# Three reorderings in a two-block transformer kernel: copies of tile 18 ahead of the heads' root, the last rotary join behind a head's low half, and the sums of x4 one tile further ahead

## The chip, the cores and the metric

The kernel runs on one core of one Trainium2 chip. The metric is the device time of one execution in microseconds (us). Five engines work side by side, each in its own program order, and meet through semaphores: PE (TensorE; its weight loads are shown apart as PEld), DVE (VectorE), ACT (ScalarE), POOL (GpSimd) and SP (SyncE, which issues most DMAs).

## The reference, cut to what matters

Two blocks follow each other on an input of 512 tokens by 1024 columns, all in float32: a gated block with a convolution and a feed-forward layer, and a block with two kinds of attention. The change lies in the second block.

```python
h = rmsnorm(x, g_pre_mix)
q_a, k_a, v_a, q_i, k_i, w_i, q_d, k_d, v_d = split(h @ w_in)
q_a, k_a = apply_rope(q_a), apply_rope(k_a)          # 8 heads of 64
o_a = dsa_attention(q_a, k_a, v_a, q_i, k_i, w_i)     # softmax over the 128 best keys
o_d = diff_attention(q1, q2, k1, k2, v_d, lam)        # 4 heads of 128
o_d = rmsnorm(o_d, g_diff_sub) * (1 - lam_init)       # per head: a root, a factor
x = x + rmsnorm(concat(o_a, o_d) @ w_out, g_post_mix) # this sum is x4
h = rmsnorm(x, g_pre_mlp)
u = relu(h @ w_up)
x = x + rmsnorm((u * u) @ w_down, g_post_mlp)
```

## The kernel before, in words

**Layout and precision.** Activations lie transposed: eight tiles k = 0..7 of 128 partitions by 512 tokens. Each operand of a large product is split into a high part (`xh`, `wh`) and a low part (`xl`, `wl`), so that one product becomes three matmuls (lines L728 to L730, helper `three`). ACT makes the high halves of activations, DVE the low halves, POOL most halves of the weights. Each engine's program is written out by hand; no scheduler moves anything.

**The attention steps.** Attention runs over 32 tiles, 16 of the differential heads (4 heads by 4 token blocks) and 16 of the sparse heads (4 pairs of heads by 4 token blocks). All engines walk through steps n = -2..32. In step n PE issues the scores of tile n+2 (L1179), a piece of some projection (L728 to L730), the transposes of tile n's probabilities (L1193, "turn"), and the product with the values of tile n-1 (L1221 or L1217). The turned tile lies in two PSUM banks, which ACT copies out in `keep_turned(n)` (L1703); PE may turn tile n+1 only into banks that are copied out. DVE does `normalise(n)` (L2533, L2534) and `shift(n+2)` (L2505), ACT the exponentials of tile n+2 (L1688).

**The heads' root.** A finished differential head needs its root of the mean square: PE sums (L826, L828), ACT takes the root in `head_roots` (L1720), which needs another activation table than the exponential and so a table load before and one behind it, DVE inverts in `head_factors` (L2540), PE spreads the factor over the partitions in `norm_spread` (L849), DVE multiplies (L2573), ACT makes the high half (L1730), DVE the low half (L2551). Heads 2 and 3 share one root; head 3's spread waits for head 2's low half, since both use one PSUM bank.

**The rotary moves.** The q and k of the sparse heads are rotated on DVE in groups g. The last one, g = 9, holds half of k (`ka`, head pairs 2 and 3). `rope_even(9)` (L2402) and `rope_odd(9)` (L2408) write the two halves of `ropey`; when the second is there, SP moves the result to its place by eight DMAs, since it must change partitions:

```python
            def move_rope(g, dst, m):

                sp.wait_ge(rope_ready, g + 1)
...
                        sp.dma_start(dst[p0:p0 + 32, 2 * m + hh // 2], ropey[32 * hh:32 * hh + 32, g % 2, part]
                                     ).then_inc(rope_moved[g % 2], 16)
```

PE asks for these moves in `scores`, ahead of the scores of tile 24 (`DIFF_TILES + 2 * TB`), which it issues in step 22 (L1179), for all eight DMAs of every group:

```python
                if n in (DIFF_TILES, DIFF_TILES + 2 * TB):
                    for half_moved in rope_moved:
                        pe.wait_ge(half_moved, 16 * 8 * (4 if n == DIFF_TILES else 5))
```

**The output projection's pieces.** `out2_piece` puts parts of `out2` between the tiles from step 19 on. Piece 3, the second one of step 21, multiplies head 3 and waits for its low half.

**x4.** Behind the attention, DVE builds x4 tile by tile in three rotating PSUM banks: `x4_scale(k)` (an L1843 multiply), `x4_sum(k)` (L2639), `x4_low(k)` (L1862). ACT makes the high half (L1774), a copy (L1770) and a square (L1410). PE's `several` takes tile k in nine matmuls, six with the high half (L786, L787) and then three with the low half (L794).

Of the kernel before, what the change touches and what calls it, by code (L numbers as in the profile page):

```python
# [35 lines left out]
KT = D // P  # L36
# [50 lines left out]
E_QK = E_VA + 4  # L87
# [40 lines left out]
def tile_of(n):  # L128

    if n < DIFF_TILES:  # L130
        return True, n // TB, n % TB
    return False, (n - DIFF_TILES) // TB, n % TB
# [16 lines left out]
def turns_to(n):  # L149

    return n + 1 if n < DIFF_TILES else DIFF_TILES + 2 * (n - DIFF_TILES + 1)


def turns_of(n):

    return range(1 if n < DIFF_TILES else 2)
# [61 lines left out]
def build(nc, a):  # L218
    ctx = ExitStack()
    with ctx:  # L220
# [1154 lines left out]
        def _(act):  # L1375
# [304 lines left out]
            def exp(n):  # L1680

                diff, h, tb = tile_of(n)
                N = (tb + 1) * P
                for e in range(2):
                    slot = 2 * (n % 3) + e
                    act.wait_ge(shifted, 2 * n + e + 1)
                    total = sums0[:, n:n + 1] if diff and e == 0 else soft[:, 8 + slot:9 + slot]
                    A(probs[slot][:, 0:N], probs[slot][:, 0:N], ACT.Exp, scale=-1.0, bias=soft[:, slot:slot + 1],  # L1688
                      accum_out=total).then_inc(exp_done, 1)

            def keep_turned(n):

                diff, h, tb = tile_of(n)
                N = (tb + 1) * P
                if n >= 2:
                    act.wait_ge(pv_done, n - 1)
                else:
                    act.wait_ge(score_step, 24)
                if n == DIFF_TILES:
                    act.wait_ge(pv_done, DIFF_TILES)  # L1700
                for e in turns_of(n):
                    act.wait_ge(turned, turns_to(n - 1) + e + 1)
                    A(pT[n % 2][e][:, 0:N], bank[turn_bank[e]][:, 0:N], ACT.Copy).then_inc(pT_ready, 1)  # L1703

            def keep_output(h):

                act.wait_ge(pv_done, 4 * (h + 1))
                if h == 0:
                    act.wait_ge(ki_moved, 64)
                    act.wait_ge(rope_ready, 6)  # L1710
                if h >= 2:
                    act.wait_ge(sums_done, 6 + h)
                A(kept[h][:], bank[1 if h == 3 else 6][:], ACT.Copy).then_inc(o_kept, 1)
                act.wait_ge(o_kept, h + 1)
                A(sq[h % 2][:], kept[h][:], ACT.Square).then_inc(head_sq, 1)

            def head_roots(n):

                act.wait_ge(sums_done, n // 8 * 2 + 7)
                A(sd[:, 0:8], NB[:, 0:8], ACT.Sqrt).then_inc(sd_ready, 1)  # L1720

            def step(n):
                if 0 <= n < TILES:
                    keep_turned(n)
                if n in HIGH_AT:

                    h = HIGH_AT[n]
                    act.wait_ge(chunk_done, C_OUT2)
                    act.wait_ge(bc_used, 9 + h)
                    A(xh[:, 4 + h], kept[h][:] if h < 2 else NB[:], ACT.Copy).then_inc(xh_ready, 1)  # L1730
                ends_head = n % 4 == 0 and 1 <= n // 4 <= DIFF_HEADS
                if n == DIFF_TILES:
                    keep_output(DIFF_HEADS - 1)
                if n + 2 < TILES:
                    exp(n + 2)
                for piece in pieces_at(n):
                    o, k = divmod(piece, 4)
                    if k == 3:
                        if o % 2:
                            act.wait_ge(chunk_done, C_OUT2 + o // 2 + 1)  # L1740
                        else:
                            act.wait_ge(even_out_done, o // 2 + 1)
                        A(ym[:, o], bank[(2, 7)[o % 2]][:], ACT.Copy).then_inc(evacuated, 1)
                if ends_head and n < DIFF_TILES:
                    keep_output(n // 4 - 1)
                if n in (9, 17):
                    head_roots(n)
                if n > DIFF_TILES + TB and n % TB == 1 or n == TILES:

                    pair = (n - DIFF_TILES - 1) // TB - (n != TILES)  # L1750
                    act.wait_ge(pv_done, DIFF_TILES + TB * (pair + 1))
                    A(xh[:, pair], bank[(6, 1)[pair % 2]][:], ACT.Copy).then_inc(xh_ready, 1)
# [79 lines left out]
        def _(dve):  # L1832
# [571 lines left out]
            def rope_odd(g, out0):  # L2404
                cs = rope_tokens(g)
                dve.wait_ge(evacuated, out0 + 2)
                dve.wait_ge(rope_step, 3 * g + 3)
                V.tensor_tensor(ropey[:, g % 2, 1, cs], tmp[2][:, cs], tmb[3][:, cs], ALU.add).then_inc(rope_ready, 1)  # L2408
# [127 lines left out]
            def head_factors(b):  # L2536

                dve.wait_ge(sd_ready, 9 + b)
                dve.wait_ge(bc_done, 8 + 2 * b)
                V.reciprocal(rn[:, 0:8], sd[:, 0:8]).then_inc(rn_ready, 2)  # L2540

            def step(n):
                if 0 <= n < TILES:
                    normalise(n)
                if n in LOW_AT:
                    h = LOW_AT[n]
                    if h == 2:
                        dve.wait_ge(xl_ready, 3 * KT + 2)
                        lows[0] += 2
                    dve.wait_ge(xh_ready, lows[0] + 1)  # L2550
                    V.tensor_tensor(xl[:, 4 + h], NB[:], xh[:, 4 + h].bitcast(F32), ALU.subtract).then_inc(xl_ready, 1)  # L2551
                    lows[0] += 1
                if n in (4, 8):
                    top_max()
                if n in (-1, 5, 9):
                    top_replace()
                if n == 12:
                    top_mask()
                if n == 17:
                    qk_second(9)  # L2560
                if n == 18:
                    rope_even(9)
                if n == 19:
                    head_factors(1)
                if n + 2 < TILES:
                    shift(n + 2)
                if n == 12:
                    head_factors(0)
                if n in SPREAD_AT:

                    h = SPREAD_AT[n]
                    dve.wait_ge(bc_done, 9 + h)
                    V.scalar_tensor_tensor(out=kept[h][:] if h < 2 else NB[:], in0=kept[h][:], scalar=diff_gain[:],  # L2573
                                           in1=NB[:], op0=ALU.mult, op1=ALU.mult).then_inc(bc_used, 1)
                if n > DIFF_TILES + TB and n % TB == 2:
                    pair = (n - DIFF_TILES) // TB - 1
                    low_of(pair, bank[(6, 1)[pair % 2]][:])
# [10 lines left out]
            for n in range(-2, TILES + 1):  # L2588
                step(n)
                if n == -2:  # L2590
                    top_max()
                if n in (0, 4, 8, 13):
                    qk_first({0: 6, 4: 7, 8: 8, 13: 9}[n])
                if n in (2, 6, 10):
                    qk_second({2: 6, 6: 7, 10: 8}[n])
                if n in (3, 7, 11):
                    qk_join({3: 6, 7: 7, 11: 8}[n])
                if n == 19:
                    rope_odd(9, E_QK + 6)
            for k in range(KT // 2):  # L2600
                x3_scale(k)
            low_of(3, bank[1][:])
# [19 lines left out]
            def x4_scale(k):  # L2622

                if k == 0:
                    dve.wait_ge(bc_done, 13)
                if k >= 3:
                    dve.wait_ge(x4_kept, k - 2)
                dve.wait_ge(ym_gained, k + 1)
                mul(x4_bank[k % 3][:], ym[:, k], NB[:]).then_inc(y_scaled if k < KT - 1 else bc_used, 1)

            def x4_sum(k):

                dve.wait_ge(x3_ready, k + 1)
                out = x4_bank[k % 3][:]
                if k < KT - 1:
                    dve.wait_ge(y_scaled, k + 1)
                else:
                    dve.wait_ge(bc_used, 13)
                V.tensor_tensor(out, out, x[:, k], ALU.add).then_inc(x4_ready, 1)  # L2639
# [5 lines left out]
            x4_scale(0)  # L2645
            x4_sum(0)
            x4_scale(1)
            for k in range(KT):
                x4_low(k)
                if k < KT - 1:  # L2650
                    x4_sum(k + 1)
                if k < KT - 2:
                    x4_scale(k + 2)
            squares[0] += KT
            plain_run(C_FF2, 13, 4, pairs_of(2)[0], "pre_mlp")
            dve.wait_ge(rn_ready, 14)
# [142 lines left out]
```

## Time and profile before

| | |
|---|---|
| median of 3 runs | 1131.68 us (1131.12 to 1131.96) |
| the profiled execution's own time | 1131.43 us |
| its span in the trace | 1129.5 us |
| PE busy | 1113.7 us (99%) |
| DVE, POOL, ACT busy | 708.6, 685.0, 391.4 us |
| granted TensorE clock | 0.999 of full speed |

The span is what the trace covers; the execution's own time has 1.9 us around it. In the rows, "busy" of PE counts matmuls whose ends are modelled and which overlap; PEld, the weight loads, shows better when PE is held. Behind an instruction stands in brackets how long its engine sat idle before it and what ended that.

### The profile page before, as it was taken

How to read it: one execution, taken by the hardware profiler on the slowest of the kernel's cores; microseconds unless marked ns; L12 is line 12 of the kernel's file. 1: busy time of each engine (PE TensorE's matmuls, PEld its weight loads, DVE VectorE, ACT ScalarE, POOL GpSimd, SP SyncE). 2: the span in 40 equal slices, each digit the busy share in tenths (PEclk: the TensorE clock that was granted, in tenths of full speed). 3: DMA queues.
4: the chain of work that ended last, by engine and by line, in shares of the span. 5: the costliest groups of instructions: out<-in, count | busy, mean ns of one | idle time of the engine just before them, and what ended most of it. 6: DMA issues, size and time to landing. Idle time of an engine off the chain costs nothing.

```text
span 1129.5 us, 17246 instructions
## 1 busy us (share of the span) xinstructions
PE 1113.7 (99%) x6167; PEld 941.9 (83%) x6167; DVE 708.6 (63%) x1386; ACT 391.4 (35%) x799; POOL 685.0 (61%) x459
## 2 busy tenths in 40 slices
PE   7999999999999999999999999999999999999997
PEld 5888788998889998888778777677899888999885
DVE  4999868851148854447789777666888113885023
ACT  5134355540015531111201346655665000554012
POOL 7869947486645586666556433135857763568662
PEclk9999999999999999999999999999999999999999
DMA  7322223243313243334333232112124822235411
GB/s 251 130 76 65 85 75 94 75 142 103 100 66 111 96 152 110 93 93 149 112 112 101 83 87 68 38 57 75 58 92 134 184 94 65 93 106 181 159 52 74
DMA packets 52251, 115.54 MB, mean 102 GB/s; under 512 B 21840, under 2 KB 22480, under 8 KB 52176
## 3 DMA queue, kind: packets, MB, share of 16 engines
q1 hardware_dynamic: 31200, 105.40, 29.1%
q10 hardware_dynamic: 20976, 9.15, 3.4%
q8 instruction: 46, 0.75, 0.3%
q14 instruction: 29, 0.24, 0.1%
HBM read 105.09 MB, written 4.19 MB: 97 GB/s over the span
## 4 chain that ended last, share of the span: by engine, by line
PE 92%; DVE 5%; ACT 2%; issue 1%; DMA 0%; DVEq 0%; SPq 0%; ACTq 0%
PE bank L728 21%; PE bank L730 20%; PE bank L729 20%; PE bank L1345 5%; PE bank L1346 5%; PE bank L1344 5%; DVE bank L1952 3%; PE bank L1179 2%; PE bank L761 1%; PE bank L762 1%; PE bank L760 1%; PE bank L794 1%; PE bank L786 1%; PE bank L787 1%; PE bank L1193 1%
## 5 line engine op out<-in xcount | busy, mean ns | idle before, releaser
L543 POOL TENSOR_TENSOR wl<-raw,wh 128x1024 fp32r<-128x1024 f32 x140 | 337.5, 2411 | 11.7
L540 POOL TENSOR_SCALAR wh<-raw 128x1024 fp32r<-128x1024 f32 x140 | 150.3, 1074 | 264.8 <-PE bank L730 148.2
L728 PE MATMUL bank<-xh,wh 128*128 128x512 f32 (+2 forms) x680 | 237.7, 350 | 0.0
L730 PE MATMUL bank<-xh,wl 128*128 128x512 f32 (+2 forms) x680 | 232.5, 342 | 0.0
L729 PE MATMUL bank<-xl,wh 128*128 128x512 f32 (+2 forms) x680 | 232.2, 341 | 0.0
L728 PEld LDWEIGHTS bank<-xh,wh 128*128 128x128 f32 x680 | 128.3, 189 | 29.3 <-issue 16.4
L730 PEld LDWEIGHTS bank<-xh,wl 128*128 128x128 f32 x680 | 128.3, 189 | 14.5
L1538 ACT ACTIVATE wh<-bank 128x512 fp32r<-128x512 f32 x96 | 52.2, 596 | 252.5 <-DVE bank L2197 109.0
L729 PEld LDWEIGHTS bank<-xl,wh 128*128 128x128 f32 x680 | 128.4, 189 | 13.0 <-issue 0.2
L728 PE MATMUL bank<-uh,wh 128*128 128x512 f32 x288 | 112.8, 392 | 0.0
L730 PE MATMUL bank<-uh,wl 128*128 128x512 f32 x288 | 112.1, 389 | 0.0
L729 PE MATMUL bank<-ul,wh 128*128 128x512 f32 x288 | 112.1, 389 | 0.0
L729 PE MATMUL bank<-t_low,wh 128*128 128x256 f32 x384 | 107.6, 280 | 0.0
L730 PE MATMUL bank<-t_high,wl 128*128 128x256 f32 x384 | 107.3, 280 | 0.0
L728 PE MATMUL bank<-t_high,wh 128*128 128x256 f32 x384 | 107.2, 279 | 0.0
L1345 PE MATMUL bank<-wl,uh 128*128 128x512 f32 x240 | 93.4, 389 | 0.0
L1346 PE MATMUL bank<-wh,ul 128*128 128x512 f32 x240 | 93.4, 389 | 0.0
L1344 PE MATMUL bank<-wh,uh 128*128 128x512 f32 x240 | 93.4, 389 | 0.0
L1843 DVE TENSOR_TENSOR bank<-bank,rb 128x512 f32<-128x512 f32 x16 | 11.2, 700 | 110.9 <-PE bank L730 110.9
L2212 DVE TENSOR_TENSOR wl<-bank,wh 128x512 fp32r<-128x512 f32 x96 | 63.4, 684 | 25.3 <-ACT wh L1538 24.7
L664 POOL TENSOR_SCALAR wh<-raw 128x512 fp32r<-128x512 f32 x24 | 14.9, 622 | 102.0 <-PE bank L730 89.0
L728 PEld LDWEIGHTS bank<-t_high,wh 128*128 128x128 f32 x384 | 72.8, 189 | 0.0
(343 smaller groups left out, 2271.8 us busy)
## 6 DMA issues: line engine op xcount, KB each, us to landing
raw<-wstream SPq DMA_DIRECT2D x188, 512.0 KB, 3.5
x<-xT SPq DMA_DIRECT2D x8, 256.0 KB, 4.8
x4rows<-x_rows ACTq DMA_DIRECT2D x4, 512.0 KB, 9.6
out<-x4rows SPq DMA_DIRECT2D x8, 256.0 KB, 2.0
qd<-ropey ACTq DMA_DIRECT2D x16, 64.0 KB, 2.1
kd<-ropey ACTq DMA_DIRECT2D x16, 64.0 KB, 2.1
qa<-ropey SPq DMA_DIRECT2D x16, 64.0 KB, 2.0
ka<-ropey SPq DMA_DIRECT2D x16, 64.0 KB, 2.0
```

The source lines that it names most:

```text
L540: nc.gpsimd.tensor_scalar(wh[c][:], raw[c][:], 1.0, 1.0, ALU.mult, ALU.mult).then_inc(high_ready, 1)
L543: nc.gpsimd.tensor_tensor(wl[c][:], raw[c][:], wh[c][:].bitcast(F32), ALU.subtract).then_inc(split_ready, 1)
L728: mm(out, wh_, mh, start=start, stop=False)
L729: mm(out, wh_, ml, start=False, stop=False)
L730: return mm(out, wl_, mh, start=False, stop=stop)
L1179: mm(bank[4 + e][:, score_columns(m)], q[r, h, tb * P:tb * P + P], k[r, h, 0:(tb + 1) * P], start=True, stop=True).then_inc(scores_done, 1)
L1344: mm(out, uh[:, f, ts], wh[s][:, ws], start=f == 0, stop=False)
L1345: mm(out, uh[:, f, ts], wl[s][:, ws], start=False, stop=False)
L1346: last = mm(out, ul[:, f, ts], wh[s][:, ws], start=False, stop=f == 15)
L1538: A(wh[slot_of(p, role)][:, 512 * part:512 * part + 512], bank[7 - made % 2][:], ACT.Copy).then_inc(sum_rounded, 1)
L1952: ins = V.scalar_tensor_tensor(out=out, in0=src, scalar=w, in1=acc, op0=ALU.mult, op1=ALU.add)
L2212: V.tensor_tensor(wl[slot][:, at], bank[7 - made % 2][:], wh[slot][:, at].bitcast(F32), ALU.subtract).then_inc(sum_ready, 1)
```

## The change: what it does

It moves four things. On ACT, the root of heads 2 and 3 stood at the end of step 17 and stands in step 18 behind the copies of turned tile 18. On DVE, the inversion of that root stood ahead of `shift(21)` and stands behind it; and `rope_odd(9)` stood behind step 19 and stands in step 20, behind the low half of head 2 and ahead of `shift(22)`. In the x4 stage, `x4_sum(k)` stood behind `x4_low(k - 1)` and stands two tiles ahead, right behind `x4_scale(k)`. No instruction is added or taken away.

```diff
@@ ACT: step(n)
                 if 0 <= n < TILES:
                     keep_turned(n)
+                if n == 18:
+                    head_roots(17)
...
-                if n in (9, 17):
+                if n == 9:
                     head_roots(n)
@@ DVE: step(n)
-                if n == 19:
-                    head_factors(1)
+                if n == 20:
+                    rope_odd(9, E_QK + 6)
                 if n + 2 < TILES:
                     shift(n + 2)
-                if n == 12:
-                    head_factors(0)
+                if n in (12, 19):
+                    head_factors(n // 19)
...
-                if n == 19:
-                    rope_odd(9, E_QK + 6)
@@ DVE: x4
             x4_scale(0)
             x4_sum(0)
             x4_scale(1)
+            x4_sum(1)
             for k in range(KT):
                 x4_low(k)
-                if k < KT - 1:
-                    x4_sum(k + 1)
                 if k < KT - 2:
                     x4_scale(k + 2)
+                    x4_sum(k + 2)
```

On ACT, around the root (L1703 copies a turned tile, L1720 is the root, L1688 the exponentials):

```order
 L1688 ACTIVATE probs_123,soft<-probs_123,soft 128x512 x2
+L1703 ACTIVATE tmp_91<-bank 128x384
+L1703 ACTIVATE vd<-bank 128x384
 L1720 ACT_TABLE_LOAD
 L1720 ACTIVATE sd<-bank 128x8
-L1703 ACTIVATE tmp_91<-bank 128x384
-L1703 ACTIVATE vd<-bank 128x384
 L1688 ACT_TABLE_LOAD
```

The two copies of tile 18 went ahead of the table load and the root; both table loads are still there.

On DVE, steps 19 and 20 before the change (L2540 the inversion, L2505 shifts, L2573 head 2 times its factor, L2408 the second rotary join, L2533 and L2534 `normalise(20)`, L2551 head 2's low half):

```order
L2540 RECIPROCAL rn<-sd 128x8
L2505 ISA probs_123,soft<-bank,work 128x256
L2505 ISA soft 128x1
L2505 ISA probs_123,soft<-bank,work 128x256
L2505 ISA soft 128x1
L2573 SCALAR_TENSOR_TENSOR bank<-rb,diff_gain,bank 128x512
L2408 TENSOR_TENSOR ropey<-tmp_90,tmb_95 128x512
L2533 RECIPROCAL soft<-soft 128x1
L2534 TENSOR_SCALAR probs_151<-probs_151,soft 128x128
L2533 RECIPROCAL soft<-soft 128x1
L2534 TENSOR_SCALAR probs_152<-probs_152,soft 128x128
L2551 TENSOR_TENSOR xl<-bank,xh 128x512
```

The same place of the changed kernel, from the inversion on, where every line number is two higher:

```order
L2542 RECIPROCAL rn<-sd 128x8
L2575 SCALAR_TENSOR_TENSOR bank<-rb,diff_gain,bank 128x512
L2535 RECIPROCAL soft<-soft 128x1
L2536 TENSOR_SCALAR probs_151<-probs_151,soft 128x128
L2535 RECIPROCAL soft<-soft 128x1
L2536 TENSOR_SCALAR probs_152<-probs_152,soft 128x128
L2553 TENSOR_TENSOR xl<-bank,xh 128x512
L2410 TENSOR_TENSOR ropey<-tmp_90,tmb_95 128x512
L2507 ISA probs_123,soft<-bank,work 128x384
```

The four shift instructions went ahead of the inversion, and the join moved past five instructions, among them the low half that waits for ACT.

On DVE, the start of the x4 stage before (L1843 scales, L2639 sums, L1862 makes the low half):

```order
L1843 TENSOR_TENSOR bank<-ym,bank 128x512
L2639 TENSOR_TENSOR bank<-bank,x 128x512
L1843 TENSOR_TENSOR bank<-ym,bank 128x512
L1862 SCALAR_TENSOR_TENSOR xl<-bank,cols,xh 128x512
L2639 TENSOR_TENSOR bank<-bank,x 128x512
L1843 TENSOR_TENSOR bank<-ym,bank 128x512
L1862 SCALAR_TENSOR_TENSOR xl<-bank,cols,xh 128x512
```

and in the changed kernel:

```order
L1845 TENSOR_TENSOR bank<-ym,bank 128x512
L2639 TENSOR_TENSOR bank<-bank,x 128x512
L1845 TENSOR_TENSOR bank<-ym,bank 128x512
L2639 TENSOR_TENSOR bank<-bank,x 128x512
L1864 SCALAR_TENSOR_TENSOR xl<-bank,cols,xh 128x512
L1845 TENSOR_TENSOR bank<-ym,bank 128x512
L2639 TENSOR_TENSOR bank<-bank,x 128x512
L1864 SCALAR_TENSOR_TENSOR xl<-bank,cols,xh 128x512
```

Each sum now stands directly behind the scaling whose result it reads, and the first low half has one more sum ahead of it.

## Rows read from the trace of the kernel before

**Rows 1.** The page: busy time of each engine, share of the span, instructions.

```profile
PE 1113.7 (99%) x6167; PEld 941.9 (83%) x6167; DVE 708.6 (63%) x1386; ACT 391.4 (35%) x799; POOL 685.0 (61%) x459
```

**Rows 2.** PE's waits, whole span: total us, times, longest us.

```profile
PE bank L786 <- ACT xh L1418: 5.6, 1, 5.6
PE bank L1193 <- ACT tmp L1703: 0.5, 1, 0.5
```

**Rows 3.** Timeline, ACT: start us, us, instruction, [idle before <-releaser].

```profile
702.80 1.28 ACT L1720 ACT_TABLE_LOAD   x1
704.10 0.18 ACT L1720 ACTIVATE sd<-bank 128x8 f32<-128x8 f32 x1
704.17 0.48 ACT L1703 ACTIVATE tmp<-bank 128x384 f32<-128x384 f32 x1
704.54 0.50 ACT L1703 ACTIVATE vd<-bank 128x384 f32<-128x384 f32 x1
705.06 1.28 ACT L1688 ACT_TABLE_LOAD   x1
...
708.09 0.59 ACT L1730 ACTIVATE xh<-bank 128x512 fp32r<-128x512 f32 x1
```

**Rows 4.** Timeline, DVE, steps 19 to 21.

```profile
703.62 0.49 DVE L2534 TENSOR_SCALAR probs<-probs,soft 128x512 f32<-128x512 f32 x1
704.36 0.20 DVE L2540 RECIPROCAL rn<-sd 128x8 f32<-128x8 f32 x1 [0.25 <-ACT sd L1720]
...
707.00 0.69 DVE L2408 TENSOR_TENSOR ropey<-tmp,tmb 128x512 f32<-128x512 f32 x1
...
708.79 0.69 DVE L2551 TENSOR_TENSOR xl<-bank,xh 128x512 fp32r<-128x512 f32 x1 [0.31 <-ACT xh L1730]
709.40 0.55 DVE L2505 CUSTOM_DVE_ANT_0 probs<-bank,work 128x384 f32<-128x384 f32 x1
...
711.92 0.69 DVE L2551 TENSOR_TENSOR xl<-bank,xh 128x512 fp32r<-128x512 f32 x1
```

**Rows 5.** Timeline, PE's weight loads, steps 19 to 22.

```profile
704.77 0.85 PEld L1193 LDWEIGHTS bank<-ident,probs 128*128 128x128 f32 x8 [0.91 <-DVE probs L2534]
705.59 0.47 PEld L849 LDWEIGHTS bank<-ident,rn 128*128 128x128 f32 x4
...
709.53 0.41 PEld L849 LDWEIGHTS bank<-ident,rn 128*128 128x128 f32 x4 [0.71 <-DVE xl L2551]
...
712.77 0.19 PEld L728 LDWEIGHTS bank<-xh,wh 128*128 128x128 f32 x1
...
714.59 0.52 PEld L1179 LDWEIGHTS bank<-ka,qa 64*128 64x128 f32 x8 [0.17 <-issue]
```

**Rows 6.** Timeline, SP's queue: the move of group 9.

```profile
707.72 4.95 SPq L469 DMA_DIRECT2D ka<-ropey  x8
```

**Rows 7.** The same move by line: duration ns, first and last start; landing.

```profile
L469 SPq DMA_DIRECT2D ka<-ropey x8: 512/591/592, 707.7 to 712.1; - x8
...
DMA to landing us min/median/max: 1.9/2.0/2.0
```

**Rows 8.** SP's queue by line, 679 to 685 us: landing of group 8's moves.

```profile
DMA to landing us min/median/max: 1.9/2.0/3.0
```

**Rows 9.** Timeline of the x4 stage.

```profile
781.57 0.69 DVE L1843 TENSOR_TENSOR bank<-ym,bank 128x512 f32<-128x512 f32 x1 [0.74 <-PE bank L849]
...
782.37 0.70 DVE L2639 TENSOR_TENSOR bank<-bank,x 128x512 f32<-128x512 f32 x1
...
784.87 0.19 PEld L787 LDWEIGHTS bank<-xh,wl 128*128 128x128 f32 x1
...
785.10 0.65 PEld L794 LDWEIGHTS bank<-xl,wh 128*128 128x128 f32 x3
...
785.94 0.75 DVE L1862 SCALAR_TENSOR_TENSOR xl<-bank,cols,xh 128x512 fp32r<-128x512 f32 x1 [0.16 <-ACT xh L1774]
...
786.61 0.69 DVE L2639 TENSOR_TENSOR bank<-bank,x 128x512 f32<-128x512 f32 x1
...
787.20 0.68 DVE L1843 TENSOR_TENSOR bank<-ym,bank 128x512 f32<-128x512 f32 x1
...
798.62 0.75 DVE L1862 SCALAR_TENSOR_TENSOR xl<-bank,cols,xh 128x512 fp32r<-128x512 f32 x1 [0.76 <-ACT xh L1774]
```

## The prediction, made before the changed kernel ran

> **What bounds the kernel now.** The page comes first: PE is busy 1113.7 us, 99% of the span [rows 1]. A microsecond taken from another engine is therefore worth nothing unless PE stands waiting for it, and a microsecond by which PE is held comes out at the end almost whole. The view of waits shows how few holds are left: one of 5.6 us at the start, where the first input is fetched, and otherwise half a microsecond here and there [rows 2]. So I read the timelines around the places of the change and asked for each instruction of PE what releases it and how long before PE got there that was ready. Since matmuls overlap in the rows, I use the weight loads (PEld), whose idle time shows a hold plainly.
>
> In steps 18 to 20 a chain through ACT holds PE twice. ACT works without a break: table load, root, two copies of tile 18, table load, exponentials, two copies of tile 19, head 2's high half [rows 3]. PE's loads first sit idle 0.91 us before tile 19 is turned [rows 5]. That row names DVE, but DVE was done at 703.62 + 0.49 = 704.11 us [rows 4]; last came the bank that ACT's first copy of tile 18 frees at 704.17 + 0.48 = 704.65, and the view of waits says so too [rows 2, 3]. It waits again, 0.71 us, for head 2's low half at 709.53, and that low half started when ACT's high half was done [rows 3 to 5].
>
> **The root behind the copies.** ACT's own sum over the moved piece: before, from 702.80 to the end of the second table load at 705.06 + 1.28 = 706.34, 3.54 us. After: copies 0.37 (the distance of the two starts) + 0.50, table load 1.28, root 0.18, table load 1.28, with gaps of 0.02 as between these rows, together 3.67 us [rows 3]. The difference of 0.13 us is that a copy could start 0.07 us behind the root, while a table load starts only when the instruction before it has ended. So the exponentials, the copies of tile 19 and head 2's high half come 0.13 us later: the high half at 708.22, the low half at 708.92, PE's second spread at 709.66.
>
> What does PE win? It can turn tile 19 when DVE's second half is there, about 704.2 instead of 704.77. But next in its order is the spread of head 2's factor. The root now starts at 702.80 + 0.87 + 0.02 + 1.28 + 0.02 = 704.99, the inversion 0.26 us behind its start as before (704.36 - 704.10), so at 705.25, and it lasts 0.20: the spread can start near 705.49, where it started at 705.59 [rows 3 to 5]. The shift that now stands ahead of the inversion is done by then: DVE is free from 704.11 on, and even two shifts of 384 columns would take 1.1 us at 0.55 each, these have 256 [rows 4]. The hold of 0.91 us is thus not removed, it moves 0.6 us down PE's program; and the 0.1 us won is lost again at the second spread, which ACT's chain decides. Worth of this part: 0.13 us lost.
>
> **The join behind the low half.** This decides the forecast. `rope_odd(9)` started at 707.00 [rows 4]. It will start one instruction behind the low half: 708.92 + 0.61 (the distance 708.79 to 709.40 in the same rows) = 709.53, so 2.53 us later. Three things follow.
>
> First, everything DVE has behind it moves by 0.61 + 0.13 = 0.74 us: `shift(22)`, head 3's product, and head 3's low half, which ended at 711.92 + 0.69 = 712.61. PE asks for it at 712.77 [rows 4, 5], a margin of 0.16 us. It will end at 713.35 while PE gets there at 712.90, so PE is held about 0.5 us more.
>
> Second, SP's eight DMAs hang on the join. Before, the first was issued at 707.72, 0.72 us behind the join's start, the last at 707.72 + 4.95 - 0.59 = 712.08, 4.36 us behind the first, and each lands 2.0 us behind its issue: the last at 714.1 [rows 6, 7]. PE needs all of them for the scores of tile 24 and issues these at 714.59 after no more than 0.17 us of idle time that the view calls issue, as at many such places [rows 5]. The margin was therefore about 0.5 us, and it was never seen as a wait. After: 709.53 + 0.72 + 4.36 + 2.0 = 716.61 for the last landing, and some 0.06 us for PE to go on: 716.67. Against 714.59 that is **2.08 us later**. The 0.13 and 0.5 us from above do not add up with it: they let PE arrive at about 715.0 and wait 1.6 us there instead of 2.2. SP issues the eight in one piece, with nothing of its weight loads between them [rows 6].
>
> Third, could it be caught up? Behind the wait, DVE and ACT will stand ready, but PE is not waiting for them in the steps after; only such a wait could give time back. POOL and the weight DMAs run ahead of PE and do not set it. So 2.08 us stay.
>
> **The sums of x4.** Before, DVE's low half of tile k is followed by the sum of k+1 (0.67 us behind its start), the sum releases ACT's high half, and this the next low half: a loop of (798.62 - 785.94) / 6 = 2.113 us [rows 9]. Each low half waits 0.16 us for it, so this loop, and not DVE's own work, sets the pace. PE's nine matmuls go at 0.23 us each in this stage (784.87 to 785.10), 2.08 us. So PE is held about 0.03 us per tile. After, high halves come early, and DVE's own pace counts: low to scale 0.67, scale to sum 0.80, sum to next low 0.61. The 0.80 is read from 781.57 to 782.37, where the sum reads what the scaling just wrote; a pair without that stands 0.59 to 0.61 apart (786.61 to 787.20, and 708.79 to 709.40) [rows 4, 9]. That makes 2.08 us, no slower than PE. The first low half comes later, with one dependent sum in front: 781.57 + 0.80 + 0.61 + 0.80 + 0.61 = 784.39, done at 785.14 against PE's load at 785.10: a hold of 0.1 us. The seven following tiles give back 0.03 each, 0.2 us; together with the first tile's change-over 0.1 to 0.2 us are won. I take 0.15. The bounds: 0.3 us lost, if the dependent pairs cost 0.05 us more in each of seven tiles, and 0.3 us won, if PE is never held.
>
> The Trainium skill, "VectorE: DVE Perf Modes", section "The DRAIN you can't avoid", states that between chained vector instructions "the semaphore costs nothing extra here". By that, the dependent pair would take 0.61 us like any other, DVE's pace would be 1.89 us, and this term 0.3 us instead of 0.15. The row of 0.80 speaks against it for this pair, and I go by the row.
>
> **Sum.** 1131.43 us is the profiled execution's own time, 1129.5 of span and 1.9 around it. Plus 2.08, minus 0.15: 1133.36. The median of the runs stands 0.25 us above that execution, so I forecast 1131.68 + 1.93 = **1133.6 us**. What a measurement of this kernel can tell from no change is about 0.2%, 2.26 us: slower means above 1133.94. The forecast is a real loss that just stays within that bound.
>
> **The rivals.**
> - *The moves are hidden* (1 in 10). PE would have to get to tile 24 later than I reckon, or DMAs land faster. For it: no wait on a DMA shows anywhere near before. Against: the margin is two subtractions from rows, and the shift is five times as large. Then the 0.13 and 0.5 us remain: 1131.68 + 0.63 - 0.15 = 1132.2 us.
> - *Slower by more than the bound* (about 1 in 4 in all). The move of group 8 had one DMA that took 3.0 us instead of 2.0 [rows 8]. If the last DMA of group 9 is such a one, its later landing goes straight to PE: 1133.6 + 1.0 = 1134.6 us. It decides from 0.35 us of lateness on. Against: group 9's eight DMAs all took 1.9 to 2.0 us, [rows 7]. That gives 1 in 10; the rest is my own error of some 0.4 us on the main case.
> - *Faster* (1 in 20). The turn of tile 19, up to 0.6 us earlier, holds if the factor's spread comes as early too, which needs a root on ACT ahead of 704.5; and the moves are hidden. With x4's 0.3 that is 0.9 us: 1130.8 us. It decides where the inversion starts before 704.4, and ACT's order all but excludes that. Only with further gains that I see no row for would it pass 0.2%.
>
> **How the numbers follow.** Main case 0.75, with a range of its own of 1133.1 to 1134.2; hidden 0.10; a late landing 0.10; faster 0.05. The range goes from 1132.0, which takes in the hidden case, to 1134.7, which takes in the late landing; outside are the faster case and the tails. Of the main case, 0.15 lies above 1133.94, and of the late landing nearly all: slower 0.25. Faster by over 0.2% gets 0.03, and the rest, 0.72, lies within.
>
> **What the changed kernel's profile would show.** The join (now L2410) starts near 709.5 us and SP's eight moves near 710.25. PEld's L1179 of tile 24 starts near 716.7 with an idle time of about 1.8 us before it, and the view of waits has a line of PE or PEld on a DMA of `ka` that was not there. The turn of tile 19 starts near 704.2, and the first L849 behind it at 705.5 with an idle time of 0.6 us. The piece of `out2` at 712.77 starts near 713.4. In the x4 stage the loads of L794 stand 2.08 to 2.10 us apart. The forecast is wrong if L1179 of tile 24 shows no wait, if the join starts earlier than 709, or if the last landing lies more than 0.4 us from 716.6.

## The result, and the profile after

The changed kernel takes 1133.13 us (median of 22 runs, 1132.77 to 1134.47), before 1131.36 us (22 runs, 1131.08 to 1131.96): 1.77 us more, a ratio of 1.0016 with a 95% interval of 1.0010 to 1.0022. The forecast was 1133.6 us, 1.93 us more. Nineteen of the 22 runs lie between 1132.77 and 1133.47 us; three stand apart at 1134.28 to 1134.47; the paragraph on the rivals, near the end, comes back to them.

The page of the changed kernel: span, and busy time by engine, which answer to [rows 1]:

```profile
span 1131.5 us, 17246 instructions
PE 1114.3 (98%) x6167; PEld 942.7 (83%) x6167; DVE 709.2 (63%) x1386; ACT 391.8 (35%) x799; POOL 684.2 (60%) x459
```

The engines do the same work as before in a span 2.0 us longer. Not all of the 2.0 is the change's. A weight load ahead of every edit tells how the two traces stand to each other; before, then after:

```profile
699.87 0.30 PEld L826 LDWEIGHTS bank<-scaled_eps,ident 128*128 128x128 f32 x2 [0.17 <-issue]
```

```profile
700.22 0.30 PEld L826 LDWEIGHTS bank<-scaled_eps,ident 128*128 128x128 f32 x2 [0.17 <-issue]
```

This execution was 0.35 us late already, so 0.35 us comes off every time of it that is set against the rows of before. By the two profiled executions the change costs 1133.44 - 1131.43 - 0.35 = 1.66 us.

PE's weight loads in the changed kernel, timeline, answering to [rows 5]:

```profile
704.25 1.02 PEld L1193 LDWEIGHTS bank<-ident,probs 128*128 128x128 f32 x8
705.77 0.41 PEld L849 LDWEIGHTS bank<-ident,rn 128*128 128x128 f32 x4 [0.50 <-issue]
...
709.86 0.41 PEld L849 LDWEIGHTS bank<-ident,rn 128*128 128x128 f32 x4 [0.90 <-DVE xl L2553]
...
713.59 0.19 PEld L728 LDWEIGHTS bank<-xh,wh 128*128 128x128 f32 x1 [0.54 <-DVE xl L2553]
...
716.87 0.55 PEld L1179 LDWEIGHTS bank<-ka,qa 64*128 64x128 f32 x8 [1.76 <-issue]
```

There are four things to see. The 0.91 us idle before the turn of tile 19 is gone. But 0.50 us of idle time stands now before the first spread, where there was none, and 0.90 us before the second, where 0.71 stood. A hold of 0.54 us for head 3's low half is new. And the scores of tile 24 start at 716.87 - 0.35 = 716.52 instead of 714.59, 1.93 us later, behind 1.76 us of idle time. The view calls this idle time "issue": it names no DMA as what ended it. The rows of the move itself show what did, SP's queue as a timeline and then by line:

```profile
710.43 4.95 SPq L469 DMA_DIRECT2D ka<-ropey  x8
```

```profile
L469 SPq DMA_DIRECT2D ka<-ropey x8: 513/591/592, 710.4 to 714.8; - x8
...
DMA to landing us min/median/max: 1.9/2.0/2.0
```

The last of the eight is issued at 710.43 + 4.95 - 0.59 = 714.79 and lands 2.0 us later, at 716.79; PE goes on at 716.87. DVE and ACT around it, from the timelines:

```profile
709.11 0.69 DVE L2553 TENSOR_TENSOR xl<-bank,xh 128x512 fp32r<-128x512 f32 x1 [0.96 <-ACT xh L1732]
709.72 0.68 DVE L2410 TENSOR_TENSOR ropey<-tmp,tmb 128x512 f32<-128x512 f32 x1
```

```profile
702.94 0.19 ACT L1688 ACTIVATION_READ_ACCUMULATOR probs<-probs,soft 128x1 f32 x1
703.03 0.47 ACT L1703 ACTIVATE tmp<-bank 128x384 f32<-128x384 f32 x1
703.40 0.48 ACT L1703 ACTIVATE vd<-bank 128x384 f32<-128x384 f32 x1
703.89 1.28 ACT L1720 ACT_TABLE_LOAD   x1
705.19 0.18 ACT L1720 ACTIVATE sd<-bank 128x8 f32<-128x8 f32 x1
705.38 1.28 ACT L1688 ACT_TABLE_LOAD   x1
```

The join starts 0.61 us behind the low half. It stands behind 0.96 us in which DVE does nothing but wait for ACT.

### The profile page after: what moved, and what is told of

Same layout as the page of the kernel before. It is cut to its first block, busy times and chain, and to the rows that moved or that the text cites. A ratio compares the mean times of both kernels' runs of the same rounds, so it can differ in the third digit from the quotient of the medians.

```text
span 1131.5 us, 17246 instructions
## 1 busy us (share of the span) xinstructions
PE 1114.3 (98%) x6167; PEld 942.7 (83%) x6167; DVE 709.2 (63%) x1386; ACT 391.8 (35%) x799; POOL 684.2 (60%) x459
## 4 chain that ended last, share of the span: by engine, by line
PE 91%; DVE 5%; issue 1%; ACT 1%; DMA 0%; DVEq 0%; SPq 0%; ACTq 0%
PE bank L728 20%; PE bank L730 20%; PE bank L729 20%; PE bank L1346 5%; PE bank L1344 5%; PE bank L1345 5%; DVE bank L1954 3%; PE bank L1179 2%; PE bank L794 1%; PE bank L786 1%; PE bank L787 1%; PE bank L760 1%; PE bank L762 1%; PE bank L761 1%; PE bank L1193 1%
```

## The experiments

Each experiment was timed side by side with the kernel before, which had a median of 1131.68 us in the first set (33 runs, experiments 1 to 4), 1131.61 in the second (30, experiments 5 to 8), 1131.54 in the third (21, experiments 9 and 10). The interval of each ratio reaches about 0.09%, 1.0 us, to either side. What is smaller than that is read from the traces; the medians can only support it.

**1. The join alone.** Only these lines on the kernel before:

```diff
+                if n == 20:
+                    rope_odd(9, E_QK + 6)
                 if n + 2 < TILES:
                     shift(n + 2)
...
-                if n == 19:
-                    rope_odd(9, E_QK + 6)
```

> Only the second rotary join moves behind head 2's low half; root and x4 stay as before. If the moves of group 9 are what PE waits for, the join starts at 708.79 + 0.61 = 709.4 us, the last of the eight DMAs lands near 716.5, and the scores of tile 24 start near 716.5 instead of 714.6: about 1.9 us more than before, 1133.3 us. The rival, that only DVE's later shift and head 3's later low half hold PE, gives 0.5 us, 1131.9 us, and no idle time ahead of the scores of tile 24.

Measured: 1133.96 us (11 runs, 1133.16 to 1135.14), ratio 1.0023 (1.0014 to 1.0032). PE's weight load of tile 24's scores:

```profile
716.65 0.55 PEld L1179 LDWEIGHTS bank<-ka,qa 64*128 64x128 f32 x8 [1.75 <-issue]
```

The join alone brings the whole loss, with the idle time at the forecast place. The rival of the low half alone would have ended at 1131.9 us. Six runs stand at 1133.16 to 1133.96, around 1133.56 us, which is 1.9 us more than before as expected; five stand at 1134.76 to 1135.14, and they lift the median.

**2. The root alone.** The two edits of `head_roots` and the two of `head_factors`, nothing else.

> Only the root of heads 2 and 3 moves behind the copies of tile 18, with the inversion behind the shift; join and x4 stay as before. By the sum of ACT's own work PE's second spread starts 0.13 us later and nothing else changes: 1131.5 us. The rival, that the earlier turn of tile 19 gives PE time that stays, gives up to 0.6 us less: 1130.8 us.

Measured: 1131.63 us (11 runs), ratio 1.0 (0.9991 to 1.0009). Nothing measurable, either way. The 0.6 us rival falls; whether 0.1 us is won or lost can't be told from runs, but the trace tells it:

```profile
703.82 1.02 PEld L1193 LDWEIGHTS bank<-ident,probs 128*128 128x128 f32 x8
705.36 0.41 PEld L849 LDWEIGHTS bank<-ident,rn 128*128 128x128 f32 x4 [0.51 <-issue]
...
709.45 0.41 PEld L849 LDWEIGHTS bank<-ident,rn 128*128 128x128 f32 x4 [0.91 <-DVE xl L2553]
...
714.51 0.52 PEld L1179 LDWEIGHTS bank<-ka,qa 64*128 64x128 f32 x8 [0.17 <-issue]
```

The turn of tile 19 starts 0.95 us earlier than in [rows 5] (of which this execution is 0.07 early as a whole), and at tile 24 nothing is left of it: 714.51 + 0.07 = 714.58 against 714.59. The hold moved past the turn, as forecast.

**3. The sums of x4 alone.** Only the four lines of the x4 stage.

> Only the sums of x4 move. The changed kernel's trace has PE's low-half loads 2.054 us apart where they stood 2.117 apart: if that is the sums' doing alone, this kernel is 0.4 us faster than before, 1130.95 us. The forecast's term was 0.15 us, 1131.2 us. If the gain in the changed kernel's trace was given back later, no change: 1131.36 us.

Measured: 1131.14 us (11 runs, 1130.82 to 1131.89), 0.54 us under before, ratio 0.9995 (0.9986 to 1.0004). The interval takes in no change, so the gain is read from the trace. PE's loads of the low halves, first and last tile:

```profile
785.65 0.58 PEld L794 LDWEIGHTS bank<-xl,wh 128*128 128x128 f32 x3
...
800.00 0.64 PEld L794 LDWEIGHTS bank<-xl,wh 128*128 128x128 f32 x3
```

That is (800.00 - 785.65) / 7 = 2.05 us a tile, as in the changed kernel. Before, the same loads stand (799.92 - 785.10) / 7 = 2.117 us apart, and DVE's loop in [rows 9] takes 2.113. From the first load of the stage to the first behind it, it is 800.68 - 784.32 = 16.36 us against 16.77 before: 0.41 won.

**4. The changed kernel without the join's move.**

> The changed kernel with the join alone put back behind step 19. If the join carries the whole loss, what is left is root and x4: 0.13 lost and 0.4 won, 1131.1 us, and no idle time ahead of the scores of tile 24. If the root's part carries some of the loss, as the rival has it, it stays above 1131.5 us.

Measured: 1131.12 us (11 runs, 1130.73 to 1131.44), ratio 0.9996 (0.9987 to 1.0005), with 0.17 us of idle time before the scores of tile 24, as before the change. Its median is 2.0 us under the changed kernel's. By the medians the parts add up: 2.28 - 0.05 - 0.54 = 1.69 us from experiments 1 to 3, against 1.77 for all together. That it is so close is partly luck, since five of 11 runs stand in the upper group in experiment 1 and three of 22 in the changed kernel; with the lower groups alone it is 1.88 - 0.59 = 1.29 against 1.71, which the intervals of 1.0 us allow too.

**5. The join later still.** The changed kernel with

```diff
-                if n == 20:
-                    rope_odd(9, E_QK + 6)
                 if n + 2 < TILES:
                     shift(n + 2)
+                if n == 20:
+                    rope_odd(9, E_QK + 6)
```

> The changed kernel with the join one step further back, behind shift(22), which takes DVE 0.95 us. If the time follows the join through the eight DMAs, one for one, the last landing and the scores of tile 24 come 0.95 us later than in the changed kernel: 0.95 us more than its 1133.1 us, 1134.1 us, while head 3's low half stays where it is. If the loss comes from head 3's low half, no change from 1133.1 us.

Measured: 1135.57 us (8 runs), ratio 1.0031 (1.0020 to 1.0042). The median is 2.4 us above the changed kernel where 0.95 was expected. But the runs fall in two groups: two at 1133.97 and 1133.98, 0.9 us above the 1133.07 of the changed kernel's lower nineteen and so as expected, and six at 1135.32 to 1135.63. The profiled execution took 1135.62 us. The new idle time is there:

```profile
717.50 0.55 PEld L1179 LDWEIGHTS bank<-ka,qa 64*128 64x128 f32 x8 [2.70 <-issue]
```

2.70 - 1.76 = 0.94 us more: PE's wait follows the join one for one. The rest of the loss lies behind it. The view of stretches, first two long ones and then three short ones (us; busy time and count of PE, PEld, DVE, ACT, POOL; granted clock; DMA share; GB/s):

```profile
716.00:720.00 4.00, 2.47 (x12) 1.84 (x13) 1.40 (x7) 1.58 (x4) 0.00 (x0) 0.83 0.13 33
720.00:724.00 4.00, 4.00 (x22) 3.02 (x21) 1.61 (x7) 1.28 (x5) 0.00 (x0) 0.74 0.00 0
```

```profile
718.00:719.00 1.00, 1.00 (x7) 0.60 (x5) 0.43 (x5) 0.00 (x0) 0.00 (x0) 0.84 0.00 0
719.00:720.00 1.00, 1.00 (x3) 0.74 (x3) 0.96 (x5) 0.00 (x0) 0.00 (x0) 0.50 0.00 0
722.00:723.00 1.00, 1.00 (x9) 0.69 (x9) 0.01 (x1) 0.28 (x1) 0.00 (x0) 0.95 0.00 0
```

The granted clock is 0.83 and then 0.74 of full speed, where it is 1.00 in the same stretches of the kernels before and changed. By the microsecond it is still 1.00 while PE is idle and until 718, then 0.84, 0.50 in each of 719 to 722, 0.95 behind that, and 1.00 again. What is missing from full speed there adds up to 0.16 + 3 x 0.50 + 0.05 = 1.71 us, and the upper group stands 1.6 us above the lower. The matmuls there, from PE's timeline, the first being the scores of tile 24:

```profile
717.53 0.93 PE L1179 MATMUL bank<-ka,qa 64*128 64x128 f32 x8 [2.49 <-issue]
...
719.18 0.63 PE L730 MATMUL bank<-xh,wl 128*128 128x512 f32 x1
719.60 0.63 PE L728 MATMUL bank<-xh,wh 128*128 128x512 f32 x1
720.03 0.63 PE L729 MATMUL bank<-xl,wh 128*128 128x512 f32 x1
```

The last three start 0.43 us apart instead of 0.23: the lower of the two levels, 1.2 GHz. The matmuls themselves had been idle for 2.49 us; the 2.70 is the idle time of the loads. So there is an expensive kind of run which the DMAs' landing does not explain; all eight landed after 2.0 us here too.

**6. The join ahead of head 2's low half.** The changed kernel with `rope_odd(9, E_QK + 6)` in step 20 in front of the low half, where DVE waits.

> The changed kernel with the join one step forward, ahead of head 2's low half, where DVE stands idle 0.96 us for ACT. Nothing behind it gets later, and the join starts some 0.9 us later than before the change instead of 2.5. The margin of the moves was about 0.45 us, so PE should wait 0.5 us for them; with 0.4 us won in the x4 stage: 1131.7 us where before is 1131.6. The rival, a delay by DVE's order alone, gives the full gain of x4: 1131.2 us.

Measured: 1131.40 us (11 runs, 1131.06 to 1132.17), ratio 0.9998 (0.9989 to 1.0007). PE is idle 0.47 us before the scores of tile 24, of which 0.17 is usual:

```profile
715.77 0.55 PEld L1179 LDWEIGHTS bank<-ka,qa 64*128 64x128 f32 x8 [0.47 <-issue]
```

A hold of 0.3 us, where 0.5 was expected: against the weight load ahead of the edits the join starts 0.73 us later than before the change and not 0.9, which overdraws a margin of 0.43. Head 3's low half holds nobody. The median lies between the two readings of the expectation, 0.2 to 0.3 us from either; the trace decides for the wait.

**7. The even half's moves early.** The changed kernel, and in `move_rope` for g = 9 only, the four DMAs of the even half are issued first, behind a wait for `rope_even`, and the four of the odd half behind the join:

```diff
-                sp.wait_ge(rope_ready, g + 1)
+                if g < 9:
+                    sp.wait_ge(rope_ready, g + 1)
...
-                for hh in range(4):
-                    for part in range(2):
+                for part, hh in [(p, q) for q in range(4) for p in range(2)] if g < 9 else \
+                        [(p, q) for p in range(2) for q in range(4)]:
+                        if g == 9 and hh == 0:
+                            sp.wait_ge((rope_step, rope_ready)[part], (3 * g + 3, g + 1)[part])
```

> The changed kernel, with group 9's four moves of the even half issued as soon as that half is there, some 8 us earlier, and only four behind the join. The join stays late. The last landing comes four issues of 0.63 us earlier, 2.5 us, and so ahead of PE: no idle time at the scores of tile 24. Left are the hold of about 0.5 us for head 3's low half and x4's 0.4: 1131.6 us where before is 1131.6. Whatever the DMAs do to the spread of single runs should be gone as well: no runs 1.3 us above the others. If the late join costs by another way, 1133.1 us remain.

Measured: 1131.50 us (11 runs, 1131.19 to 1131.78), ratio 0.9999 (0.9990 to 1.0008): 1.6 us under the changed kernel with the join as late as there, and no run stands apart. The hold for head 3's low half is still there, the idle time before the scores is back at 0.17 us (all lines stand three lower in this kernel):

```profile
713.05 0.19 PEld L731 LDWEIGHTS bank<-xh,wh 128*128 128x128 f32 x1 [0.54 <-DVE xl L2556]
...
714.74 0.52 PEld L1182 LDWEIGHTS bank<-ka,qa 64*128 64x128 f32 x8 [0.17 <-issue]
```

This is the sharpest test: the programs of PE, DVE and ACT are untouched, and only the times at which SP issues the moves differ.

**8. Both.** Experiments 6 and 7 together.

> Both: the join ahead of head 2's low half, and the even half's moves early. Neither head 3's low half nor the moves are late, so what is left is the gain of x4 and of the root's order: 0.5 us under before, 1131.1 us where before is 1131.6, like the changed kernel with the join put back.

Measured: 1130.97 us (11 runs, 1130.62 to 1131.33), ratio 0.9995 (0.9986 to 1.0004) to before. By its median it is the best of all, 0.64 us under before, and 2.2 under the changed kernel; its interval to before takes in no change.

**9. PE kept busy ahead of the wait, join behind shift(22).** Experiment 5's kernel with two products of constants, added work that no result uses, ahead of PE's wait:

```diff
             def step(n):

+                if n == 22:
+                    for _ in range(2):
+                        mm(NB[:], ones[:], mask[:], start=True, stop=True)
                 if n + 2 < TILES:
                     scores(n + 2)
```

> The kernel with the join behind shift(22), and two products of constants (ones times mask, 128x512, nobody reads them) on PE ahead of the scores of tile 24, where PE stood idle 2.7 us. In the x4 stage three such products kept PE busy 2.7 us, so two fill some 1.8 us of the idle time. If the runs at 1135.6 us come from TensorE's clock going down to the 1.2 GHz level behind the idle time (granted clock 0.83 and 0.74 in the eight microseconds behind it, in the profile of one such run), they are gone and all runs stand near 1134.0 us. If they come from late DMA landings, they stay: PE waits for the same moves.

Measured: 1134.01 us, all eleven runs between 1133.81 and 1134.57; not one at 1135.3 or above, where there had been six of eight. PE waits for the same moves and resumes at the same time, 717.51 against 717.50. By the weight loads it is idle for 1.37 us before that instead of 2.70; by the matmuls, which show what the two products fill, for 0.57 us instead of 2.49:

```profile
714.99 1.98 PE L1264 MATMUL bank<-mask,ones 128*128 128x512 f32 x4
717.55 0.93 PE L1179 MATMUL bank<-ka,qa 64*128 64x128 f32 x8 [0.57 <-issue]
```

```profile
717.51 0.55 PEld L1179 LDWEIGHTS bank<-ka,qa 64*128 64x128 f32 x8 [1.37 <-issue]
```

The granted clock of 720 to 724 us is 1.00. So the 1.6 us of the upper group are the clock's, and without PE's idle time they do not come. That idle time alone does not decide it: two of the eight runs of experiment 5 had no such loss. What decides between runs of one kernel is not shown.

**10. The same with the join alone.** Experiment 1's kernel with one such product.

> The join alone moved (root and x4 as before), with one such product ahead of the scores of tile 24, where PE stood idle 1.75 us; it fills about 0.9 us. Five of eleven runs of that kernel stood 1.3 us above the others. If the clock is the cause, those are fewer or gone and the median comes down to about 1133.6 us; if it is not, about half of the runs stay near 1135 us.

Measured: 1133.72 us (11 runs, 1133.11 to 1134.66). Nine runs lie at 1133.11 to 1133.81, two at 1134.33 and 1134.66; without the product five of eleven stood at 1134.76 or above. The matmuls are idle for 0.48 us before the scores instead of 1.54. The result goes the expected way, but eleven runs are few, and two runs remain above the others whose cause is not shown: their mean granted clock, 0.999, is no lower than the others'. In experiment 1 the clock does not settle it either: 0.996 to 0.998 in the five upper runs, 0.997 to 0.999 in the six lower ones.

## Why the prediction was right

**The number.** Forecast were 1133.6 us, measured 1133.13, 0.5 us less. 0.32 us of that is the starting point: the kernel before takes 1131.36 us by its 22 runs and not the 1131.68 of three. The rest is the change itself, 1.77 us by the medians and 1.66 by the traces where 1.93 was forecast. By the traces the terms are 1.93 us lost at the moves (forecast 2.08) and 0.37 won in the x4 stage (forecast 0.15), and some 0.1 us more lost, which no term names.

**The bound and the place.** That a hold of PE comes out at the end whole is confirmed by experiments 4 and 7, which take the hold away and with it 2.0 and 1.6 us of the median. One sign did not come: the view of waits has no line of PE on a DMA of `ka`. It lists the hold under "issue".

**The root behind the copies.** The mechanism held: the turn of tile 19 earlier, the hold moved down to the spreads, nothing won at the end. The turn came at 704.25 - 0.35 = 703.90 and not at 704.2: its first loads did not wait for DVE's second half, which ended at 703.98 + 0.49 - 0.35 = 704.12. The term was mis-sized. I took 0.13 us lost; in experiment 2 the second spread starts at 709.45 + 0.07 = 709.52 against 709.53, so nothing. I had started the copies at 702.80, the table load's start. Before the change the instruction ahead of the table load was this:

```profile
702.59 0.19 ACT L1688 ACTIVATION_READ_ACCUMULATOR probs<-probs,soft 128x1 f32 x1
```

The table load started 0.21 us behind the start of that reading of the accumulator, at its end. In the changed kernel the copy starts 0.09 us behind it (702.94 to 703.03), while it still runs. The 0.12 us that the copy gains ahead of the root make up for the 0.13 lost behind it.

**The join.** Forecast: join at 709.53, last landing 716.61, scores of tile 24 at 716.67, some 1.8 us of idle time, 2.08 us lost. Measured, with the 0.35 taken off: 709.37, 716.44, 716.52, 1.76 us, 1.93 lost. The difference of 0.15 is nearly all the root's term again, which stood in this chain. Experiment 5 moved the join by 0.95 and PE's start by 0.94; experiment 6 moved it forward and the hold shrank to 0.3; experiment 7 left the join and removed the hold. The hold for head 3's low half was forecast at 0.5 us and is 0.54, and as forecast it does not add up with the wait for the moves: in experiment 7, where no such wait follows, the trace has the hold of 0.54 us and the median is 0.4 to 0.5 us above experiments 4 and 8.

**The sums of x4.** This term was the furthest off in proportion: 0.15 us won by forecast, and by the traces more than my upper bound of 0.3. PE's loads of the stage, the first of it and the first behind it, before:

```profile
783.84 0.19 PEld L786 LDWEIGHTS bank<-xh,wh 128*128 128x128 f32 x1 [0.56 <-ACT xh L1774]
...
800.61 0.19 PEld L728 LDWEIGHTS bank<-xh,wh 128*128 128x128 f32 x1
```

and in the changed kernel, with the last tile:

```profile
786.19 0.19 PEld L786 LDWEIGHTS bank<-xh,wh 128*128 128x128 f32 x1 [0.56 <-ACT xh L1776]
...
787.52 0.59 PEld L794 LDWEIGHTS bank<-xl,wh 128*128 128x128 f32 x3
...
799.85 0.65 PEld L794 LDWEIGHTS bank<-xl,wh 128*128 128x128 f32 x3
800.53 0.19 PEld L786 LDWEIGHTS bank<-xh,wh 128*128 128x128 f32 x1
...
801.90 0.64 PEld L794 LDWEIGHTS bank<-xl,wh 128*128 128x128 f32 x3
802.59 0.19 PEld L728 LDWEIGHTS bank<-xh,wh 128*128 128x128 f32 x1
```

16.77 us before, 16.40 after: 0.37 won. The first low half holds PE for 0.07 us more (787.52 - 786.19 against 785.10 - 783.84), as forecast; the seven tiles behind it give back 0.063 each and not 0.03. The step that failed is "PE's nine matmuls go at 0.23 us each in this stage (784.87 to 785.10), 2.08 us", with that pace taken as the same before and after. In tiles 2 to 8 the last five high-half loads stand on average 0.234 us apart before and 0.228 after; nine of these are 2.10 and 2.05 us. So only some 0.02 us a tile is the hold that went away, and the rest is PE's pace itself. Why that changed is open.

What sets the pace now is DVE, as its timeline in the changed kernel shows:

```profile
787.38 0.68 DVE L1845 TENSOR_TENSOR bank<-ym,bank 128x512 f32<-128x512 f32 x1
788.17 0.70 DVE L2639 TENSOR_TENSOR bank<-bank,x 128x512 f32<-128x512 f32 x1
788.78 0.74 DVE L1864 SCALAR_TENSOR_TENSOR xl<-bank,cols,xh 128x512 fp32r<-128x512 f32 x1
789.44 0.68 DVE L1845 TENSOR_TENSOR bank<-ym,bank 128x512 f32<-128x512 f32 x1
...
799.05 1.60 DVE L1864 SCALAR_TENSOR_TENSOR xl<-bank,cols,xh 128x512 fp32r<-128x512 f32 x2
```

0.79 + 0.61 + 0.66 = 2.06 us a tile, equal to the distance of PE's low-half loads, (801.90 - 787.52) / 7 = 2.054. Each of the first seven of these starts 0.05 or 0.06 us behind the end of its low half, for instance 789.58 behind 788.78 + 0.74 = 789.52. But PE has little in hand. The last two low halves follow each other directly and are done at 799.05 + 1.60 = 800.65, 1.25 us ahead of PE, and its last round, 799.85 to 801.90, still takes 2.05 us. In the eight traces with this order the last round takes 1.95 to 2.07 us, so a faster DVE would win little here.

The dependent pair does cost 0.79 us and the independent one 0.61, so for this pair the row was right to go by, against the rule of the Trainium skill ("VectorE: DVE Perf Modes", "The DRAIN you can't avoid") that the semaphore costs nothing extra. The page measured that on chained copies.

**The rivals.** That the moves are hidden is excluded by the 1.76 us. "Slower by more than the bound" came true in three of 22 runs, and what lay behind it in the forecast, a late landing, is seen in no trace with the join late: there the eight moves land after 1.9 to 2.1 us. (In experiments 7 and 8 one of the four early moves took 2.9 and 2.6 us, and nothing waited for it.) What experiment 5 shows instead is a mechanism that I had not named, TensorE's clock behind the idle time; there it rests on the granted clock and on experiment 9. For the three upper runs of the changed kernel itself it is likely, not shown: their mean granted clock is 0.996, and all others' is 0.997 to 0.999, but none of the three left rows. The faster rival needed the inversion before 704.4; it started at 705.45 - 0.35 = 705.10, so ACT's order did exclude it.

## What to carry to other kernels

When a producer is moved past one instruction, follow its result through the DMA queue to the last landing and compare that with the time at which the consumer gets there: a margin of 0.5 us shows in no view of waits, and once it is overdrawn the view can call the hold "issue" and name no DMA. Put such work where its engine already waits, ahead of the waiting instruction and not behind it (experiment 6: a hold of 0.3 us instead of 1.6), or issue the part that is ready on its own (experiment 7: no hold). And do not read an engine's own pace from a stretch in which it is held once a round.

## What was not expected of the hardware

- **An idle time of PE that ends in a slow clock.** In experiment 5 PE's matmuls stood idle for 2.49 us before the scores; six of eight runs cost 1.6 us more, and in the profiled one the clock went down to 1.2 GHz. It did so only about a microsecond after the matmuls had begun again. With the idle time cut to 0.57 us at the same place none of eleven runs cost that much. The Trainium skill, "TensorE: Matmul & The Clock Gate", section "Part 1: The HAM clock gate (the "warmup" mystery)", gives 1.2 GHz as the clock of an idle TensorE; the trace agrees in the level, but here the clock fell when the idle time was over. With 1.54 us idle in the changed kernel three of 22 runs stood apart, so a wait may have a price beyond its length, and not in every run.
- **In the x4 stage PE's loads stand 0.231 to 0.234 us apart in the four traces with the old order of the sums, where each tile begins with a short hold, and 0.226 to 0.229 in the eight with the new one**, with the same shapes. Why is open.
- **A table load starts at the end of the accumulator's reading, 0.21 us behind its start; a copy starts 0.09 us behind it.** That makes a copy ahead of a table load cheaper by 0.12 us than one behind it.
